# RWKV preparation with part of its elementwise work on GpSimd, in a changed order of pieces, on one Trainium2 core

## The reference, cut to what matters

```python
near = (u[t - 1] + u[t + 1])                  # zero rows outside, and at the seam
x    = u[t] + mu * (0.5 * near - u[t])        # token shift
r, k, v = x[0:512], x[512:1024], x[1024:1536]
kk   = k * kk_w;  kk = kk / norm_per_head(kk)
w[d] = sigmoid(w0[d] + tanh(x[1536 + ...]) @ w2[d])      # two directions d
a[d] = sigmoid(a0[d] + x[1664 + ...] @ a2[d])
kd[d]   = k * (1 + (a[d] - 1) * ka)
dots    = sum_per_head((kd[0] + kd[1]) * (r * rk))       # "bonus" is r * rk
# filters: two sine layers of 64 rows, a product with w3 and a decay, a transform (matmuls)
```

## Time and profile before

| what | value |
|---|---|
| median of 3 runs | 4884.5 us |
| the profiled execution's own time | 4883.0 us |
| its span, first to last instruction | 4881.3 us |
| mean granted TensorE clock (share of full) | 0.911 |
| TensorE matmul busy | 4150.2 us (85%) |
| VectorE busy | 2600.9 us (53%) |
| ScalarE busy | 1489.8 us (31%) |
| GpSimd busy | 685.9 us (14%) |
| this stage | from about 2721 us to about 3035 us of the span |

### The profile page before, as it was taken

One profiled execution on the slowest core, in us unless ns is written; L12 is line 12 of the kernel. 1 busy time (PEld: TensorE's weight loads), 2 busy tenths in 40 slices (PEclk: granted clock), 3 DMA queues, 4 the chain that ended last, 5 costly groups with the idle time before them and its releaser, 6 DMA issues. The chain is left out here.

```text
span 4881.3 us, 74471 instructions
## 1 busy us (share of the span) xinstructions
PE 4150.2 (85%) x28954; PEld 3446.2 (71%) x28954; DVE 2600.9 (53%) x4866; ACT 1489.8 (31%) x3127; POOL 685.9 (14%) x774
## 2 busy tenths in 40 slices
PE   5999999767899999599995576798875799989978
PEld 3899888556688877499995332687764699965646
DVE  3567775565333348611106687677764325646745
ACT  2233232643222235311103233233433311133423
POOL 1111111221000000000002102000012114423321
PEclk8999999778899999799997678799987899999998
DMA  4444432441211134412212465444434334553334
GB/s 160 159 145 144 139 129 87 179 155 65 57 52 43 43 117 162 144 67 84 78 54 96 145 244 215 115 116 109 131 84 138 123 105 172 183 155 96 99 100 138
DMA packets 430694, 589.34 MB, mean 121 GB/s; under 512 B 166297, under 2 KB 317202, under 8 KB 428772
## 3 DMA queue, kind: packets, MB, share of 16 engines
q1 hardware_dynamic: 382425, 418.15, 27.9%
q0 software_dynamic: 46336, 164.57, 9.0%
q10 hardware_dynamic: 1616, 2.36, 0.1%
HBM read 429.41 MB, written 155.57 MB: 120 GB/s over the span
## 5 line engine op out<-in xcount | busy, mean ns | idle before, releaser
L320 PE MATMUL g_in_g_acc<-g_in_g_whi,g_in_hi 128*128 128x444 f32 (+4 forms) x960 | 357.1, 372 | 14.9 <-DVE g_in_g_wlo L310 9.9
L321 PE MATMUL g_in_g_acc<-g_in_g_wlo,g_in_hi 128*128 128x444 f32 (+4 forms) x960 | 346.3, 361 | 0.0
L322 PE MATMUL g_in_g_acc<-g_in_g_whi,g_in_lo 128*128 128x444 f32 (+4 forms) x960 | 345.6, 360 | 0.0
L196 PE MATMUL g_even_acc<-g_even_w_hi,h_hi 128*128 128x384 f32 (+1 forms) x960 | 317.2, 330 | 19.4 <-DVE g_even_w_lo L238 19.4
L198 PE MATMUL g_even_acc<-g_even_w_lo,h_hi 128*128 128x384 f32 (+1 forms) x960 | 317.1, 330 | 0.0
L199 PE MATMUL g_even_acc<-g_even_w_hi,h_lo 128*128 128x384 f32 (+1 forms) x960 | 316.9, 330 | 0.0
L320 PE MATMUL g_odd_g_acc<-g_odd_g_whi,h_hi 128*128 128x344 f32 (+3 forms) x816 | 264.0, 324 | 30.8 <-DVE g_odd_g_wlo L310 17.0
L321 PE MATMUL g_odd_g_acc<-g_odd_g_wlo,h_hi 128*128 128x344 f32 (+3 forms) x816 | 262.3, 321 | 0.0
L1597 DVE SCALAR_TENSOR_TENSOR up_cv<-up_acc,up_taps,up_cv 128x1023 f32<-128x1023 f32 x88 | 112.8, 1282 | 280.2 <-ACT up_cv L1573 273.0
L322 PE MATMUL g_odd_g_acc<-g_odd_g_whi,h_lo 128*128 128x344 f32 (+3 forms) x816 | 261.7, 321 | 0.0
L214 DVE COPY g_even_o_buf<-g_even_acc 128x384 f32<-128x384 f32 (+1 forms) x60 | 32.1, 535 | 399.0 <-PE g_even_acc L199 399.0
(11 more groups left out here) (579 smaller groups left out, 9987.2 us busy)
## 6 DMA issues: line engine op xcount, KB each, us to landing
down_raw<-in_w_down SPq DMA_DIRECT2D x66, 512.0 KB
g_in_m_w<-in_ada_w SPq DMA_DIRECT2D x24, 1024.0 KB, 5.4
up_w_buf<-in_w_up SPq DMA_DIRECT2D x44, 512.0 KB
U2p<-g_even_o_buf POOLq DMA_DIRECT2D x11, 1920.0 KB, 7.8
g_odd_x<-U3p SPq DMA_DIRECT2D x24, 768.0 KB
g_even_w_buf<-in_even_w_in SPq DMA_DIRECT2D x11, 1536.0 KB
g_in_m_w<-in_w_ada SPq DMA_DIRECT2D x16, 1024.0 KB, 6.2
prep_near<-U2p SPq DMA_DIRECT2D x18, 896.0 KB
```

What stands on the lines that cost most here:

```text
L196: mm = pe.matmul(o, hi[:, k, tt], w_hi[:, par, k, :wd], start=k == 0, stop=not split and k == kc - 1)
L320: pe.matmul(bank[:, :wd], hi[:, k, tt], w_hi[:, st % 2, k, :wd], start=k == 0, stop=False)
L321: pe.matmul(bank[:, :wd], hi[:, k, tt], w_lo[:, st % 2, k, :wd], start=False, stop=False)
L322: op = pe.matmul(bank[:, :wd], lo[:, k, tt], w_hi[:, st % 2, k, :wd], start=False, stop=k == KC - 1)
```

## The change

- GpSimd takes over from VectorE the neighbours' sum (new piece `near`), the product with mu (new piece `damp`), `bonus`, and the key sum with its product with bonus (new piece `keys`).
- The pieces stand in a new order: `near` of tile t + 2 behind `mix` of tile t + 1; `shift` of tile t + 1 at the start of tile t, ahead of `okk` and `lora_out`; `damp` right behind `shift`; `dots` behind the fourth slot.
- `sine` 0 stands ahead of `shift` 0, `sine` 1 ahead of `mix` 0.
- New semaphores `nears`, `diff`, `damped`, `dirs` and `keys` tie the two engines together.

```diff
     def order():
         yield "front", 0
+        yield "near", 0
+        yield "sine", 0
         yield "shift", 0
+        yield "damp", 0
+        yield "near", 1
+        yield "sine", 1
         yield "mix", 0
-        yield "sine", 0
         yield "low", 0
         yield "norm", 0
-        yield "sine", 1
         yield "lora", 0
...
             yield "slot", SLOTS * t
+            if more:
+                yield "shift", t + 1
+                yield "damp", t + 1
             yield "bonus", t
             yield "okk", t
             yield "lora_out", t
-            if more:
-                yield "shift", t + 1
             yield "slot", SLOTS * t + 1
             if more:
                 yield "mix", t + 1
                 yield "low", t + 1
                 yield "norm", t + 1
+            if t + 2 < NTA:
+                yield "near", t + 2
             yield "slot", SLOTS * t + 2
             yield "dirs", t
             if more:
                 yield "lora", t + 1
+            yield "keys", t
+            yield "slot", SLOTS * t + 3
             yield "dots", t
-            yield "slot", SLOTS * t + 3
...
         # GpSimd
+                up = near[:, par, 0]
+                if what == "near":
+                    pool.wait_ge((s.near_even, s.near_odd)[par], (t // 2 + 1) * NEAR + (2 * DMA if t >= NTC - 1 else 0))
+                    pool.tensor_tensor(up, up, near[:, par, 1], ALU.add)
+                    pool.drain()
+                    pool.sem_inc(s.nears, 1)
+                if what == "damp":
+                    if t == 0:
+                        pool.wait_ge(s.mu, DMA)
+                    pool.wait_ge(s.diff, t + 1)
+                    pool.tensor_tensor(up, up, mu_r[:], ALU.mult)
+                    pool.drain()
+                    pool.sem_inc(s.damped, 1)
+                if what == "bonus":
+                    if t == 0:
+                        pool.wait_ge(s.rows_in, 2 * DMA)
+                    pool.wait_ge(s.mixed, t + 1)
+                    pool.tensor_tensor(bonus[:], x[:, par, 0:512], rowsb["rkr"][:], ALU.mult)
+                if what == "keys":
+                    pool.wait_ge(s.dirs, t + 1)
+                    if t:
+                        pool.wait_ge(s.k_done, t)
+                    pool.tensor_tensor(ksum[:], od[:, par, 0, 1], od[:, par, 1, 1], ALU.add)
+                    pool.drain()
+                    pool.tensor_tensor(ksum[:], ksum[:], bonus[:], ALU.mult)
+                    pool.drain()
+                    pool.sem_inc(s.keys, 1)
...
         # VectorE
                 if what == "shift":
-                    dve.wait_ge((s.near_even, s.near_odd)[par], (t // 2 + 1) * NEAR + (2 * DMA if t >= NTC - 1 else 0))
-                    dve.tensor_tensor(up, up, near[:, par, 1], ALU.add)
-                    dve.drain()
+                    dve.wait_ge(s.nears, t + 1)
                     dve.wait_ge((s.x_even, s.x_odd)[par], (t // 2 + 1) * DMA)
-                    dve.scalar_tensor_tensor(up, up, 0.5, x[:, par], ALU.mult, ALU.subtract)
-                    dve.drain()
-                    if t == 0:
-                        dve.wait_ge(s.mu, DMA)
-                    dve.tensor_tensor(up, up, mu_r[:], ALU.mult)
+                    dve.scalar_tensor_tensor(up, up, 0.5, x[:, par], ALU.mult, ALU.subtract).then_inc(s.diff, 1)
                 if what == "mix":
-                    dve.drain()
+                    dve.wait_ge(s.damped, t + 1)
                     dve.tensor_tensor(x[:, par], x[:, par], up, ALU.add)
...
-                if what == "bonus":
-                    dve.tensor_tensor(bonus[:], r, rowsb["rkr"][:], ALU.mult)
...
                     dve.drain()
+                    dve.sem_inc(s.dirs, 1)
                 if what == "dots":
-                    dve.tensor_tensor(ksum[:], od[:, par, 0, 1], od[:, par, 1, 1], ALU.add)
-                    dve.drain()
-                    dve.tensor_tensor(ksum[:], ksum[:], bonus[:], ALU.mult)
-                    dve.drain()
+                    dve.wait_ge(s.keys, t + 1)
                     dve.tensor_reduce(dots[:, par], ksum[:].rearrange("p (h d) -> p h d", d=HD), AX_X, ALU.add).then_inc(s.k_done, 1)
```

More of the change, by code:

```diff
@@ L2284, in in_order @@
                 part("spec", k)
-    with stage(nc, "prep", "const", "rows_in", "mu", "x_even", "x_odd", "near_even", "near_odd", "mixed", "keyed", "root", "tanh", "turned", "tT",
+    with stage(nc, "prep", "const", "rows_in", "mu", "x_even", "x_odd", "near_even", "near_odd", "nears", "diff", "damped", "mixed", "dirs", "keys", "keyed", "root", "tanh", "turned", "tT",
                "ring", "freed", "lora_b", "sig", "scaled_out", "k_done", "rv_even", "rv_odd", "stored_even", "stored_odd",
@@ L2518, in part @@
                 par = t % 2
-                r, k = x[:, par, 0:512], x[:, par, 512:1024]
+                k = x[:, par, 512:1024]
                 if what == "sine":
```

## The result

Changed kernel: 4948.5 us (median of 4 runs, 4946.4 to 4952.1). Kernel before, same chip: 4882.6 us (4 runs, 4877.7 to 4891.1). Ratio 1.014, 95% interval 1.0127 to 1.0153: slower by 66 us. The forecast was 4955 us. The profiled execution took 4950.6 us, its span 4948.9 us.

What follows compares the result with a forecast made beforehand. VectorE was taken as the bound, 22.7 us a tile against TensorE's 18.9. Six tiles +65, behind them +1, start +4: +70 us on the 4884.5 us median, rounded to 4955 us; range 4940 to 4970, 8 in 10 4922 to 4988.

Steps and rivals of the forecast that it cites:

- The tile: One steady tile, from the end of one `mix` to the next: 34.2 us against 22.7 us before.
- x: Ahead of `shift`, directly behind `dots`: the load of x, issued only when `dots` is done, stands open, +5.2 us a tile.
- `near` blocks `norm`: After `mix`: GpSimd's neighbours' sum takes the shared port and `norm` waits, +4.1 us a tile.
- `damp` ahead of `okk`: Behind `shift`: `damp` takes the port first, so `okk` waits until 4.1 us behind the shift instead of 0.5 us.
- rival A: `okk` gets the port first and `damp` is hidden: 3.5 us less in seven tiles, 25 us, total 4930 us; chance 0.13.
- ScalarE's copy: Behind `lora_out`: VectorE waits 3.6 us a tile for the copy of a PSUM half, which `shift` covered before.
- One-input operations: In the sine steps: 1024-column operations with one input are held up by GpSimd too; otherwise the start is 4 to 6 us shorter.
- The start: Up to `mix` 3: +4 us in all, between -5 and +15, with the filters starting 1.4 us earlier.
- Total: Whole kernel: +65 for six tiles, +1 behind them, +4 at the start, +70 us.
- B: No blocking to speak of: `near` and `damp` cost VectorE nothing, tile 26.5 us, total time 4899 us; chance 0.06.
- C: TensorE stays at its low clock and becomes the bound: tile 36.4 us, total time 4983 us; chance 0.08.
- D: VectorE's two waits fall into GpSimd's time; TensorE's 18.9 us a tile is the bound: total time 4858 us; chance 0.03.

Runs made afterwards that it cites:

- order_only: Changed kernel's new order of pieces, with all four works taken back from GpSimd to VectorE; 4936.0 us, ratio to the kernel before 1.009 to 1.0126.
- x_early: Changed kernel with the load of x issued when `dirs` ends and `bonus` has read r, instead of when `dots` ends; 4918.5 us.
- copy_first: Changed kernel with slot 4t+1 ahead of `lora_out` on every engine, so ScalarE's copy of the PSUM half stands ahead of the sigmoid; 4921.6 us.
- near_late: Changed kernel with the neighbours' sum of tile t+2 behind `dots` of tile t instead of behind `norm` of t+1; 4964.1 us.
- okk_first: Changed kernel with the three small operations of `okk` ahead of `shift` instead of behind it; 4912.5 us.
- work_only: The four works on GpSimd as in the changed kernel, but each piece placed where the kernel before had it; 4920.1 us.
- four_inc: Changed kernel with sum behind `dots`, `okk` ahead of `shift`, slot 4t+1 ahead of `lora_out`, x loaded at `dirs` end, no drain behind the sum; 4887.8 us.

## Why the prediction was right

- **The tile, 34.2 forecast, 34.2 measured** (2896.35 to 2930.56). Term by term, forecast first: `near` and `norm` 4.7 / 4.2; `dirs` 4.1 / 4.1; `keys` 3.0 / 2.8; `dots` 0.8 / 0.7; x 5.2 / 6.2; `shift` 2.0 / 1.9; `damp` and `okk` 4.7 / 4.6; `lora_out` 2.6 / 2.5; ScalarE 3.6 / 3.6; `spec_out` and `mix` 3.5 / 3.6. So the terms are right in kind, but that the sum agrees to a tenth is luck: two errors cancel, x a whole microsecond too cheap, the rest together one too dear.
- **x.** The term that was mis-sized. The loads of `near` do leave 10.5 us ahead of x, so the reason that I gave holds, but the best landing does not follow from it: it became longer than the median of before. order_only has 6.1 us at best too, with no work on GpSimd; x_early, issued ahead of the stores, has 4.6. What changed around the issue is the KS store: 0.23 us ahead of x, where before it left 2.3 us behind it. The three stores of `dots` stood as close before, and the last load there, with no load of `near` in the 13 us ahead of it, landed in 5.1 us. That points at the KS store for some 1 us; no run moves it alone. SyncE's other load behind x (L2370, 1024 KB, 2.0 us later) is not the cause: the tile before has none and waits 6.14 us.
- **`near` blocks `norm`.** Right, slightly dear: the sum ended 3.8 us behind `mix`, and GpSimd's 1792 columns take 3.95 us by themselves, not 4.1. copy_first and near_late, which move the sum away, bring `norm` to 0.69 us. The Trainium skill, "GPSIMD Engine Reference", section "4.1 Engine selection", calls GpSimd about 2 times slower than VectorE on two inputs; here it is 3.95 against 2.02.
- **`damp` ahead of `okk`.** Right; rival A (`okk` first) did not happen by itself: `okk` took 4.15 us in every tile that has a `damp`. okk_first gained 36 us where I had put 25 on A, but it does more than A says: it also hides `okk`'s own 1.1 us in the wait for x.
- **ScalarE's copy.** Right to 0.04 us; copy_first takes it away.
- **One-input operations.** 3.32 and 4.28 us for 0.69: they are held up, as I took it. The Trainium skill's rule in "SBUF — State Buffer", section "SBUF: two separate sides", that two-port modes count in, agrees with these two rows.
- **The start.** +3.7 us up to the end of `mix` 3, for +4, but by other terms. The filters began at 2767.3 (forecast 2769.3). In the tile before `mix` 3 the wait for x is 7.2 us, of which the kernel before had already paid 3.1 (below), which I had overlooked; and the sum that runs ahead of `mix` 3 holds it by 2.4 us, which I had put at nothing. So this agreement is in part luck too.

```profile
2858.57 2.02 DVE L2534 SCALAR_TENSOR_TENSOR prep_near<-prep_near,prep_x 128x1792 f32<-128x1792 f32 x1 [3.06 <-DMA prep_x<-U2p]
```

- **Total.** +65.7 for six tiles (forecast +65), +1.2 behind them (+1), +3.7 ahead (+4): 70.5 in the stage. The span grew by only 67.6, since the other stages were some 3 us shorter in this execution; that is scatter outside the change.
- **Rivals.** B falls with 4.15 us for `okk`, C with 15.15 us for 32 matmuls, D with the tile of 34.2 us.

One thing the prediction did not see and did not need: GpSimd's drains. In the changed kernel they end within 0.5 us of their operation or where nobody waits for them.

## What to carry to other kernels

Work that leaves an engine leaves its cover too: before moving a piece, list which transfers and which other engine's copies it hid, since here the order alone cost 54 us and the work alone 47. Give GpSimd only what lies beside VectorE's operations on PSUM or beside its waits. And let an operation of GpSimd that stands behind its DMA issues signal by itself instead of through a drain, which here waited until those DMAs had landed.

## What the runs showed of the hardware that was not expected

- **A drain on GpSimd lasts until GpSimd's own DMAs have landed.** After the PD store (1536 KB) it ended up to 12 us after the issue (near_late 2913.92 to 2926.03, landing at 2925.82; work_only, with a KS store behind it, 2903.89 to 2916.09, landing of the KS store at 2915.87), though the sum had ended 7.4 and 5.7 us before. In four_inc the drain of `keys` ended at 2911.34, 2.8 us behind its operation, and the KS store had landed at 2911.26. In the changed kernel the KS store had landed 2.7 us before the sum ended, and the drain ended 0.14 us behind the sum. All 52 such drains of these runs fit. The Trainium skill, "GPSIMD Engine Reference", section "4. When to use GPSIMD", says that for such a DMA two of GpSimd's cores write the descriptors; no run here shows how long that writing lasts, so whether the drain waits for the landing itself or for something that ends with it stays open.
- **The same load of 896 KB lands in 4.6 to 6.4 us, by what is in flight.** It took 4.7 us with the stores 3.3 us behind it (x_early), 6.2 us with a store 0.2 us ahead and three close behind (changed kernel), 6.4 us with the loads of `near` 4.8 us ahead (four_inc), and 4.6 us there without them.
- **A block is worth as much as its place.** The same 3.95 us of `damp` cost 3.5 us a tile ahead of `okk` and nothing beside `lora_out`.
